# Stick-breaking sums of two heads in one product per block, and other places for pool differences, gain products and first scores

## The reference

```
proj = rmsnorm(h) @ w_in            # u, qf, kf, vf, fl, qs, ks, vs
y_pool: mean of u over windows of 2, 4, 8, 16 tokens, less u, times pool_w   (4 groups of 64)
y_fox : softmax(q k^T / 8 + c_q - c_k) v, c = cumsum(log_sigmoid(fl + bias))  (6 heads of 64, causal)
y_sb  : z = q k^T / 8;  strict = key < query
        log_1m = where(strict, log_sigmoid(-z), 0)
        later  = cumsum of log_1m from the last key backwards, less log_1m
        a      = where(strict, exp(log_sigmoid(z) + later), 0);  a v          (6 heads of 64)
h = h + concat(y_pool, headnorm(y_fox), headnorm(y_sb)) @ w_out
```

## Time and profile before

| what | value |
|---|---|
| median of three runs | 937.27 us (935.64 to 938.26) |
| profiled execution | 936.92 us, span 935.2 us |
| TensorE busy | 904.7 us (97%) |
| VectorE, ScalarE, GpSimd busy | 596.3, 465.3, 94.9 us |
| mean granted TensorE clock | 0.985 of full speed |
| TensorE sums L1446, x72 | slots 10, 13, 16, from 85.79 us to 135.43 us |

### The profile page before, as it was taken

How to read it: one execution, slowest core, us unless ns; L and a number is a source line. 1 busy time by engine, 2 the same in 40 slices (tenths; PEclk the granted TensorE clock), 3 DMA queues, 4 the chain that set the end, 5 groups by cost and what they waited for, 6 DMA issues and landing times.

```text
span 935.2 us, 19567 instructions
## 1 busy us (share of the span) xinstructions
PE 904.7 (97%) x7444; PEld 867.8 (93%) x7444; DVE 596.3 (64%) x967; ACT 465.3 (50%) x742; POOL 94.9 (10%) x149
## 2 busy tenths in 40 slices
PE   8989999999999999999999999999998999999997
PEld 8878888999999998977899999999898899999996
DVE  5765446665666577545585566666879975556665
ACT  6444456543444355534664444444777644444443
POOL 4220001100000004920010000000222100000000
PEclk9998889999999999999999999999999999999999
DMA  7432223756555654732536555555344455555551
GB/s 256 158 114 68 68 86 118 244 184 202 179 182 177 203 181 133 240 96 85 192 129 201 189 188 180 179 184 199 135 136 157 158 166 192 185 190 186 180 179 46
DMA packets 44947, 152.64 MB, mean 163 GB/s; under 512 B 5860, under 2 KB 7140, under 8 KB 44900
## 3 DMA queue, kind: packets, MB, share of 16 engines
q1 hardware_dynamic: 41184, 145.52, 47.3%
q0 software_dynamic: 2912, 5.48, 1.8%
q10 hardware_dynamic: 804, 0.98, 0.3%
HBM read 148.58 MB, written 1.05 MB: 160 GB/s over the span
## 4 chain that ended last, share of the span: by engine, by line
PE 88%; DVE 8%; ACT 2%; issue 1%; DMA 1%; SPq 0%; DVEq 0%; POOL 0%; ACTq 0%
PE bank L1236 26%; PE bank L1238 25%; PE bank L1237 25%; DVE alo L864 3%; PE bank L1446 2%; PE bank L1577 2%; DVE wlo L839 1%; PE bank L1326 1%; DVE h L874 1%; PE bank L1271 1%; PE bank L1343 1%; PE bank L1668 1%; PE bank L1366 1%; ACT whi L464 1%; DMA raw<-in_slabs 1%
## 5 line engine op out<-in xcount | busy, mean ns | idle before, releaser
L1236 PE MATMUL bank<-ahi,whi 128*128 128x256 f32 (+1 forms) x1400 | 404.3, 289 | 5.2 <-DVE proj L883 2.9
L1238 PE MATMUL bank<-ahi,wlo 128*128 128x256 f32 (+1 forms) x1400 | 396.4, 283 | 0.0
L1237 PE MATMUL bank<-alo,whi 128*128 128x256 f32 (+1 forms) x1400 | 396.2, 283 | 0.0
L839 DVE TENSOR_TENSOR wlo<-raw,whi 128x1024 fp32r<-128x1024 f32 x273 | 333.5, 1230 | 32.9 <-ACT whi L464 32.6
L464 ACT ACTIVATE whi<-raw 128x1024 fp32r<-128x1024 f32 x273 | 282.2, 1050 | 119.2 <-PE bank L1238 114.5
L1236 PEld LDWEIGHTS bank<-ahi,whi 128*128 128x128 f32 x1400 | 267.1, 191 | 9.5 <-DVE proj L883 3.5
L1237 PEld LDWEIGHTS bank<-alo,whi 128*128 128x128 f32 x1400 | 267.3, 191 | 0.5
L1238 PEld LDWEIGHTS bank<-ahi,wlo 128*128 128x128 f32 x1400 | 267.2, 191 | 0.0
L1236 PE MATMUL bank<-hidhi,whi 128*128 128x256 f32 x704 | 197.4, 280 | 3.2 <-issue 2.1
L1237 PE MATMUL bank<-hidlo,whi 128*128 128x256 f32 x704 | 196.9, 280 | 0.0
L1238 PE MATMUL bank<-hidhi,wlo 128*128 128x256 f32 x704 | 196.9, 280 | 0.0
(11 more groups left out here) (198 smaller groups left out, 719.2 us busy)
## 6 DMA issues: line engine op xcount, KB each, us to landing
raw<-in_slabs SPq DMA_DIRECT2D x273, 512.0 KB, 3.4
shared<-zpad POOLq DMA_DIRECT2D x64, 35.5 KB, 3.1
shared<-in_convw POOLq DMA_DIRECT2D x4, 512.0 KB, 6.3
raw<-in_slabs SPq DMA_DIRECT2D x8, 128.0 KB, 5.7
vtok<-in_gatew POOLq DMA_DIRECT2D x2, 512.0 KB, 4.3
out<-y SPq DMA_DIRECT2D x4, 256.0 KB, 2.7
h<-in_xT ACTq DMA_DIRECT2D x3, 272.0 KB, 5.4
h<-in_xT SPq DMA_DIRECT2D x1, 272.0 KB, 3.4
```

Of the source, the lines that this page charges most:

```text
L839: dve.tensor_tensor(wlo[:, n % R, :, :], raw[:, n % R, :, :], whi[:, n % R, :, :].bitcast(F32), ALU.subtract).then_inc(lo_done, 1)
L1236: pe.matmul(dst, hi, xh, start=start, stop=False, skip_group_check=True)
L1237: pe.matmul(dst, hi, xl, start=False, stop=False, skip_group_check=True)
L1238: return pe.matmul(dst, lo, xh, start=False, stop=stop, skip_group_check=True)
```

## The change

The 24 rounded products of a pair's sums become nine. Both heads are in one product: bank one holds the first block's queries of both heads (2 x 256 columns), bank two the second and third block's (2 x 160). Six products are rounded, over the 128 wide blocks of keys; the last 16 keys are done in three fp32 products of 2 x 16 columns, from `sbs` itself. VectorE's subtractions go by bank in place of by head. `gmat` moves to slots 3 and 5, behind their splits. The pool differences move ahead of the take of column 13. The scores of slot 0 wait for `cum` alone; the wait for `cumT` goes to slot 4, that for the value copies to slot 1.

```diff
@@ the banks of the sums
+        sum_bank = (aux_bank[:, :].rearrange("p (a b) -> p a b", a=2),
+                    gemm_bank[1][:, 0:2 * (SBW - SEQ)].rearrange("p (a b) -> p a b", a=2))
@@ VectorE, columns 6 and 7
-                if n in (IN1 + 6, IN1 + 7):
-
-                    for k in range(4 * (n - IN1 - 6), 4 * (n - IN1 - 5)):
-                        dve.tensor_scalar(gmat[:, k, :], ones[:, :], gg[:, k:k + 1], None, ALU.mult).then_inc(gprod, 1)
@@ VectorE, slots
-                    for hd in range(2):
-                        ins = dve.tensor_tensor(sbz[p % 2][:, hd, :], sbz[p % 2][:, hd, :], sb_bank[hd][:, 0:SBW], ALU.subtract)
+                    for a, c0, c1 in ((0, 0, SEQ), (1, SEQ, SBW)):
+                        w = sbz[p % 2][:, :, c0:c1]
+                        ins = dve.tensor_tensor(w, w, sum_bank[a], ALU.subtract)
                     ins.then_inc(r_masked, 1)
+                if u == 6:
+
+                    dve.wait_ge(pool_d, 1)
+                    for w, buf, p0, c in ((2, win, 0, 0), (4, win2, HD, 0), (8, win, 0, 1), (16, win2, HD, 1)):
+                        ins = dve.scalar_tensor_tensor(pd[p0:p0 + HD, c, :], buf[p0:p0 + HD, c, NMETA:], 1.0 / w,
+                                                       proj[p0:p0 + HD, PU + c, NMETA:], ALU.mult, ALU.subtract)
+                    ins.then_inc(pool_d, 1)
...
-                if u == 6:
...
+                if u in (3, 5):
+                    for k in range(2 * (u - 3), 2 * (u - 3) + 4):
+                        dve.tensor_scalar(gmat[:, k, :], ones[:, :], gg[:, k:k + 1], None, ALU.mult).then_inc(gprod, 1)
@@ TensorE, sb_sums
-                for hd in range(2):
-                    for part in (sbhi, sblo):
-                        for a in range(3):
-                            for j in range(a, 3):
-                                m = P if j < 2 else NMETA
-                                c = SBC[a] + SBQ[j] - SBQ[a]
-                                ins = pe.matmul(sb_bank[hd][:, c:c + SBN[j]], (tri_r if a == j else ones_r)[0:m, :],
-                                                part[0:m, hd, SBC[j]:SBC[j] + SBN[j]],
-                                                start=(part is sbhi and j == 0), stop=False, skip_group_check=True)
+                first, second = sum_bank
+
+                def block(j, t, rows=P):
+                    return t[0:rows, :, SBC[j]:SBC[j] + SBN[j]]
+                for part in (sbhi, sblo):
+                    pe.matmul(first, tri_r[:, :], block(0, part), start=(part is sbhi), stop=False, skip_group_check=True)
+                    pe.matmul(first[:, :, SBQ[1]:], ones_r[:, :], block(1, part), start=False, stop=False, skip_group_check=True)
+                for part in (sbhi, sblo):
+                    pe.matmul(second[:, :, 0:SBN[1]], tri_r[:, :], block(1, part), start=(part is sbhi), stop=False,
+                              skip_group_check=True)
+                last = block(2, sbs, NMETA)
+                pe.matmul(first[:, :, SBQ[2]:], ones[0:NMETA, :], last, start=False, stop=True, skip_group_check=True)
+                pe.matmul(second[:, :, SBQ[2] - SBQ[1]:SBN[1]], ones[0:NMETA, :], last, start=False, stop=False,
+                          skip_group_check=True)
+                ins = pe.matmul(second[:, :, SBN[1]:], tri[0:NMETA, :], last, start=False, stop=True, skip_group_check=True)
                 ins.then_inc(r_ready, 1)
@@ TensorE, slots
                     if s == 0:
-                        pe.wait_ge(cum_t, 2)
-                        pe.wait_ge(v_ready, 2)
+                        pe.wait_ge(cum_ready, 1)
...
                 if u == 4:
+                    pe.wait_ge(cum_t, 2)
...
+                    if u == 1:
+                        pe.wait_ge(v_ready, 2)
```

## The result

The changed kernel takes 915.23 us (median of 4 runs, 914.65 to 916.70) against 937.62 us (4 runs), a ratio of 0.9775 with a 95% interval of 0.9758 to 0.9792: 22.4 us faster. The prediction was 914. The slowest of the four runs, 916.70 us, has a mean granted clock of 0.948 on record where the other three have 0.997 and 0.998, and no trace of it was kept.

What follows compares the result with a forecast made beforehand. TensorE, busy 97% of the span, was taken as the bound, with its granted clock at 0.91 in the edited slots. The terms 1.8 + 4.1 + 17.05 = 22.95 us gave 914 us, range 910 to 921.

Steps and rivals of the forecast that it cites:

- First scores: Slot 0: scores start right behind the gate sums' transposes without waiting for cumT; 1.8 us gone, bounds 1.5 and 1.9.
- its first sign: The first scores start within 0.2 us of the transposes of the gate sums.
- Pool: Around the pool products: earlier differences cut TensorE's idle time, the products and the column behind; 4.1 us gone.
- The upper bound of 4.9 us: Most that the pool part could save, against 4.1 us taken and a lower bound of 2.9.
- Sums: Three pairs: nine products take 1.7 us, 4.9 with the column or row behind; 17.05 us gone, bounds 14 and 18.
- The high end for the six: Six wide rounded sums products a pair: 1.9 us at most, with 0.14 us of its own for each product.
- The rival that it falls all the same: The clock still falls at the sums, costing 7 us in all: 921 us, 13 in 100.
- the one that wide products run no faster a column: Wide rounded sums products cost as much a column as narrow ones, 5.9 us left: 931 us, 5 in 100.
- The rival of late differences: gmat and window sums hold each other up until the pool gap is whole; 4.1 us lost: 918 us, 5 in 100.
- the rival on the slower side: The clock stays at the lower level from slot 8 through slot 18: 940 us, 2 in 100.
- What lies beside the sums: VectorE's subtraction comes at 88.0, still ends before the column; slots behind keep their inner order, nothing added.
- the prediction's upper bound: Four gain products in slot 5: 2.0 us, if they and GpSimd's window sums exclude each other.

Runs made afterwards that it cites:

- the first scores alone: The kernel before with only the waits of the first scores moved, the gain products left ahead of the copy to cumT: 933.82 us, ratio 0.9968.
- in slot 7: The changed kernel with the second four gain products in slot 7 instead of slot 5: 913.85 us, ratio 0.9757.
- two experiments: The kernel before with only the waits of the first scores moved, 933.82 us; the kernel before with only the pool differences moved, 930.47 us.
- whole rows: The changed kernel with gain products in slots 3 and 7 and the last three fp32 products over all 128 partitions: 912.80 us, ratio 0.9751.
- the other order: The kernel before with the same 24 sums products a pair, the 12 with 128 keys first, then the 12 with 16: 924.99 us, ratio 0.9882.
- the 144 wide pairs: The changed kernel with each 288 wide product of the sums as two of 144 columns, one a head: 915.85 us in one run.
- The spread products: The kernel before with the second head's 12 sums products in the middle of the column or row behind: 932.15 us, ratio 0.9951.
- the sums alone: The kernel before with only the nine sums products a pair and the subtraction by bank: 921.57 us, ratio 0.9830.

## Why the prediction was right, and where its reasons were not

**First scores: right.** 1.71 us for 1.8; the scores started 0.22 us behind the transposes, a hair over the 0.2 of its first sign. The copy of the values ended at 36.90, the column started at 37.28. That VectorE had to be rid of the gain products was not needed, as the first scores alone showed. Missed was that this gap, too, lowers the clock in some executions; in those it costs 1.5 us more.

**Pool: right, in its parts.** Idle time left 0.69 us (forecast 0 to 1.2, taken 0.5), products 1.01 (1.1), column 3.21 (3.2). The cause named was right: in slot 7 the gain products leave no gap. They took 1.72 us, inside the bounds of 0.8 and 2.0. Their move into slot 5 was thus a loss of 0.8 us, and two experiments found no use for it; a kernel with everything else of the change and the gain products left alone was not run. The upper bound of 4.9 us is 0.3 more than its parts give (3.08 + 0.5 + 1.0), which changes nothing.

**Sums: right in the total, wrong in what a product costs.** The forecast was 1.7 us for the nine products, measured 1.95. The six wide ones went nearly at the column's pace (1.17 us, low end 1.07, taken 1.3), the three in fp32 took 0.78 us, the high end, where 0.4 was taken: they did not scale with their width, as the step had it, but cost 0.24, 0.23 and 0.31 us. With whole rows, where no change of partitions stands beside them, the six take 1.08 us (79.39 to 80.47) and the three 0.58, two instructions each at some 0.10; the other 0.29 us of the 1.95 are two changes. The fp32 products are the term that was mis-sized. Their row was also read by a duration, 0.26 us a product; by the distance of starts (37.95 to 38.39 for two) it is 0.22. That the total of 4.9 us for a stretch still met 4.98 on average is partly luck: the columns and rows behind took 3.0 us, where 3.2 was taken.

The high end for the six was built on "0.14 us each are their own". That reading failed: products with 128 keys and 144 columns cost 0.06 to 0.12 us when others with 128 keys stand around them. Of the 3.4 us by which the 24 products exceed their columns at full clock (4.58 less 1.16), 1.66 went with 14 of the 16 changes between 128 and 16 partitions, and most of the rest is a least price of some 0.11 us a product, which products of 16 columns pay in full. A rule worked out afterwards from these runs gives all of them: 0.46 ns a column, but at least 0.11 us an instruction, and 0.12 us a change. It makes 2.30 us for the first 12 products before (measured 2.29), 2.92 for the 24 in the other order (2.92), 2.25 with the 144 wide pairs (2.27), 1.89 for the changed sums (1.95) and 1.65 with whole rows (1.66). So the wide products were the smaller part of what made the sums cheap: of 2.63 us a pair at full clock (4.58 to 1.95) ending the alternation gave 1.66. With the clock's part behind it, the mere order gave 10.8 us where the new sums give 15.5.

**The clock: right.** None of the three falls is left, nor the one behind the pool, and no column in the slots takes over 3.3 us. The spread products show the clock's part by itself, 2.9 us a pair in two pairs of three. The rival that it falls all the same is out; so is the one that wide products run no faster a column: 512 columns cost 0.23 us (80.75 to 80.98), 0.45 ns each. The rival of late differences came true by 0.69 us of the 3.08. Nothing of the rival on the slower side was seen.

**What lies beside the sums: right.** VectorE had no idle time before its subtraction at 82.44, which ends well before the column, and TensorE's waits in slots 10 to 17 are those of before (0.3, 0.3 and 0.6 us). The slots became 22.4 us shorter, for 23; the 0.28 us by which the rest grew are the fall told in the result.

## What to carry to other kernels

When small products cost more than their columns, read the partitions of each row beside its width: a change in the number of partitions cost 0.12 us here (1.66 for 14) to 0.15 (0.29 for two), so group products by it, or run a short contraction over all partitions with zeros behind it. Price a stretch of small products with what the clock does to it and to the work behind it, and expect scatter of 1.4 us a stretch between executions as long as a fall is there. When a step is moved off a critical wait, look at what its own engine owes the others in the new place, and at what runs beside it there: the gain products two slots later were worth 0.8 us in the timeline.

## What the runs showed of the hardware, not expected

- A rounded product over 128 keys and 144 columns costs 0.06 us (87.24 to 87.30) to 0.12 (87.30 to 87.42) among its like, and cost 0.26 (86.35 to 86.61) between products over 16 keys. A product of 16 or 32 columns costs 0.10 to 0.12 us, with 16 keys or 128.
- The Trainium skill, "TensorE: Matmul & The Clock Gate", part 2, on LDWEIGHTS, says that a load takes the time of its columns, not of its keys. The 0.11 us a product with few columns, whatever its keys, agree with it.
- The four gain products took 0.87 us alone and 1.72 us beside GpSimd's window sums, with the same instructions. They did not all become slower: the first took 0.65 us and the third 0.76, the other two 0.28 and 0.27 as alone, and the two long ones end 0.1 us behind the ends of two GpSimd instructions (59.34 and 60.22). So they stood still for GpSimd, as the prediction's upper bound assumed.
- A gap of 1.64 us at TensorE left the clock at 1.00 in the profile of before and brought it down to 0.60 over the next 4 us in another kernel with the same gap (the sums alone).
